# Token-tile order at the joints of a two-block transformer kernel on one Trainium2 core

## The reference

```python
for l in range(DEPTH):          # DEPTH = 2
    h = layer_norm(ALPHA * h + 0.5 * swiglu(h, ffn1_w_gate[l], ffn1_w_up[l], ffn1_w_down[l]), ...)
    h = layer_norm(ALPHA * h + hybrid_mixer(h, ...), ...)       # ends in merged @ w_out
    h = layer_norm(ALPHA * h + 0.5 * swiglu(h, ffn2_...), ...)
```

```python
def modulated_residual(x, c, g, w_mod, b_mod, fn):
    shift, scale, gate = split(silu(c) @ w_mod + b_mod, 3)
    return x + gate * fn(rms_norm_2(x, g) * (1 + scale) + shift)
# swiglu(x) = (silu(x @ w_gate) * (x @ w_up)) @ w_down ; a last rms_norm_2 gives the output
```

## Time and profile before

| | |
|---|---|
| three runs | 3263.46, 3270.26, 3270.85 us; median 3270.26 us |
| profiled execution | 3271.35 us, of which the traced span is 3269.6 us |
| PE busy | 2963.7 us, 91% |
| DVE busy | 1881.6 us, 58% |
| ACT busy | 1355.8 us, 41% |
| mean granted TensorE clock | 0.946 |

### The profile page before, as it was taken

How to read it: one execution, slowest core, us unless ns; L and a number is a source line. 1 busy time by engine, 2 the same in 40 slices (tenths; PEclk the granted TensorE clock), 3 DMA queues, 4 the chain that set the end, 5 groups by cost and what they waited for, 6 DMA issues and landing times.

```text
span 3269.6 us, 41313 instructions
## 1 busy us (share of the span) xinstructions
PE 2963.7 (91%) x15778; PEld 2481.8 (76%) x15778; DVE 1881.6 (58%) x2365; ACT 1355.8 (41%) x1541; POOL 47.6 (1%) x93
## 2 busy tenths in 40 slices
PE   6999898789999989878999799886899999999997
PEld 6987686589899868766987499464777877788776
DVE  6654632176776372325760354142877887778776
ACT  4431211144444122112531154121767666676664
POOL 2000010000000000000000000000000000000000
PEclk9999998889999989989999899977999999999999
DMA  7744321267587332116752365321989988899885
GB/s 255 244 160 148 107 104 54 103 226 247 193 273 245 116 113 103 54 52 222 241 205 103 116 193 165 123 73 48 330 310 334 349 321 314 317 345 341 298 311 213
DMA packets 373331, 659.57 MB, mean 202 GB/s; under 512 B 9034, under 2 KB 195256, under 8 KB 373240
## 3 DMA queue, kind: packets, MB, share of 16 engines
q1 hardware_dynamic: 373240, 658.31, 57.5%
HBM read 657.23 MB, written 1.05 MB: 201 GB/s over the span
## 4 chain that ended last, share of the span: by engine, by line
PE 77%; DVE 9%; issue 5%; DVEq 3%; ACT 2%; PEld 2%; DMA 1%; ACTq 0%; PEldq 0%; SPq 0%
PE banks L649 17%; PE banks L650 17%; PE banks L651 17%; PE banks L1076 9%; PE banks L645 3%; PE banks L1830 3%; DVE ffn_tmp L1557 2%; PE banks L1858 2%; PE banks L1233 2%; PE banks L701 1%; PE banks L773 1%; DVE expert_rest L999 1%; PEld banks L1233 1%; DVEq L1550 1%; PEld banks L1360 1%
## 5 line engine op out<-in xcount | busy, mean ns | idle before, releaser
L649 PE MATMUL banks<-ffn_arena 128*128 128x256 f32 (+1 forms) x3460 | 1169.8, 338 | 69.5 <-DVE expert_rest L999 32.9
L651 PE MATMUL banks<-ffn_arena 128*128 128x256 f32 (+1 forms) x3460 | 1152.7, 333 | 0.0
L649 PEld LDWEIGHTS banks<-ffn_arena 128*128 128x128 f32 x3460 | 664.2, 192 | 142.4 <-issue 45.6
L651 PEld LDWEIGHTS banks<-ffn_arena 128*128 128x128 f32 x3460 | 663.6, 192 | 69.8
L999 DVE TENSOR_TENSOR expert_rest<-expert_raw,ffn_arena 128x2048 fp32r<-128x2048 f32 (+1 forms) x306 | 647.8, 2161 | 118.8 <-ACT ffn_arena L865 113.6
L650 PE MATMUL banks<-ffn_arena 128*128 128x256 f32 (+1 forms) x2200 | 674.0, 306 | 0.0
L865 ACT ACTIVATE ffn_arena<-expert_raw 128x2048 fp32r<-128x2048 f32 (+1 forms) x306 | 538.1, 1809 | 261.2 <-PE banks L651 117.9
L650 PE MATMUL banks<-expert_rest,ffn_arena 128*128 128x512 f32 (+1 forms) x1224 | 468.2, 383 | 0.0
L650 PEld LDWEIGHTS banks<-ffn_arena 128*128 128x128 f32 x2200 | 425.1, 193 | 17.1
L1076 PE MATMUL banks<-HT,panel 128*128 128x256 f32 x1408 | 310.9, 382 | 2.7 <-issue 2.7
L1076 PEld LDWEIGHTS banks<-HT,panel 128*128 128x128 f32 x1408 | 267.8, 192 | 41.8 <-issue 5.9
(11 more groups left out here) (392 smaller groups left out, 2771.4 us busy)
## 6 DMA issues: line engine op xcount, KB each, us to landing
expert_raw<-in_moe_w_gate_dram SPq DMA_DIRECT2D x45, 2048.0 KB, 8.5
expert_raw<-in_moe_w_up_dram SPq DMA_DIRECT2D x45, 2048.0 KB, 7.9
expert_raw<-in_moe_w_down_dram SPq DMA_DIRECT2D x45, 2048.0 KB, 7.9
gate_w<-in_ffn_w_gate_dram SPq DMA_DIRECT2D x55, 1024.0 KB, 5.3
up_w<-in_ffn_w_up_dram SPq DMA_DIRECT2D x55, 1024.0 KB, 5.4
down_w<-in_ffn_w_down_dram SPq DMA_DIRECT2D x55, 1024.0 KB, 5.4
mod_unit<-in_mod_w_dram SPq DMA_DIRECT2D x48, 1024.0 KB, 5.2
panel<-in_w_in_dram SPq DMA_DIRECT2D x24, 2048.0 KB, 8.2
```

Of the source, the lines that this page charges most:

```text
L649: mm(out, w[0], x[0], start=start, stop=False)
L651: return mm(out, w[1], x[0], start=False, stop=stop)
```

## The change

1. `ffn_down_last` takes down panels 9 and 10 together: all of tile 0 for both panels, then all of tile 1. When tile 0's banks are complete it raises a new semaphore, `tile_done`. The output projections have the tile outside the blocks: inside a panel in the mixer and the convolution, outside both panels in attention. The drain after the first of the two panels is gone.
2. `layer_norm`, `residual`, `norm_vec`, `rms_act`, `norm_pe` and the last norm run one tile to its end before the next: tile 0 waits for `tile_done`, tile 1 for `down_done` or `mix_done`. More explicit drains stand between DVE's steps.
3. `mod_pe` writes bank 0 instead of bank 4. Ahead of a mixer it stands between the transposes of the two tiles, after the second FFN behind a wait for tile 0's norm. ACT copies the 24 columns (`mod_act`); the bias is added later, in `norm_start`.
4. `norm_start` (modulation scale and the eight diagonal tiles) moves ahead of the wait for the last products.
5. In an FFN's last step DVE does `panel_low` ahead of `unit_vec`.
6. At the convolution-to-FFN joint ACT copies the gate panel right after `mix_done`, ahead of the squares, and the high part of `HT` is made by halves inside `norm_act`.

```diff
+        def ffn_down_last(pe, n):
+            for t in range(TT):
+                for s, units, weights in ((NS - 2, unit_parts, down_parts), (NS - 1, last_unit_parts, last_down_parts)):
+                    if t == 0:
+                        pe.wait_ge(down_low, n + s + 2)
+                        pe.wait_ge(act_ready, n + s + 1)
+                    for f in range(FB):
+                        last = down_block(units, weights, f, t, False, s == NS - 1 and f == FB - 1)
+                    if t == TT - 1:
+                        last.then_inc(down_done, 1)
+                    elif s == NS - 1:
+                        last.then_inc(tile_done, 1)
...
-        def turn_h(pe, done):
+        def turn_h(pe, done, mod=None):
             for t in range(TT):
+                if t == 1 and mod is not None:
+                    mod_pe(pe, mod)
                 pe.wait_ge(norm_done, done + t + 1)
...
+        def mod_act(act, m):
+            act.wait_ge(mod_col_done, m + 1)
+            act_fn(mod_col[:, bass.ds(m * 24, 24)], banks[:, 0, 0:24], ACT.Copy)
...
         def std_act(act, m, eps):
-            act.wait_ge(var_ready, m)
-            act_fn(spread[:, :, 0], moments[:, :, 1], ACT.Sqrt, bias=eps).then_inc(std_ready, 1)
+            for t in range(TT):
+                act.wait_ge(var_ready, m * TT - TT + t + 1)
+                act_fn(spread[:, t, 0:1], moments[:, t, 1:2], ACT.Sqrt, bias=eps).then_inc(std_ready, 1)
...
-                unit_vec(dve, n, s, FB * SEQ)
                 if final:
                     panel_low(dve, n, s, down_high, down_w, last_down_parts, down_low)
-                else:
+                unit_vec(dve, n, s, FB * SEQ)
...
             for i in range(2):
                 tile = v3(panel_ready(18 + i), 0, 4, D)
-                for k in range(4):
-                    for t in range(TT):
+                for t in range(TT):
+                    for k in range(4):
...
+                    if i == 1 and t == 0:
+                        last.then_inc(tile_done, 1)
             pe.drain().then_inc(mix_done, 1)
+            pe.drain().then_inc(panel_used, 2)
...
                 ffn_pe(pe, n + NS, l * 2 + 1)
+                pe.wait_ge(norm_done, l * 6 + 7)
                 mod_pe(pe, l * 2 + 1)
...
-            def residual(j, src):
+            def residual(j, src, tile=None, whole=None):
                 dve.wait_ge(grow_ready, j + 1)
+                if j + 1 < 4:
+                    norm_start(j + 1)
                 for t in range(TT):
-                    tt(x_norm[:, t, :], src[:, t, :], gate_row[:], ALU.mult)
-                dve.drain()
-                for t in range(TT):
-                    tt(H[:, t, :], H[:, t, :], x_norm[:, t, :], ALU.add)
+                    if t == 0 and tile is not None:
+                        dve.wait_ge(tile_done, tile)
+                    if t == 1 and whole is not None:
+                        dve.wait_ge(*whole)
+                    tt(ffn_tmp[:], src[:, t, :], gate_row[:], ALU.mult)
+                    dve.drain()
+                    tt(H[:, t, :], H[:, t, :], ffn_tmp[:], ALU.add)
+                    dve.drain().then_inc(var_ready, 1)
...
-            norm_act(1)
+            act.wait_ge(mix_done, DEPTH + 1)
             gate_act(act, FFN2, 0)
-            x_high_act(act)
+            norm_act(1, True)
```

More of the change, by code:

```diff
@@ L675, in ffn_down @@
                 for t in range(width // P):
-                    for c in range(2):
-                        last = split_mm(banks[:, 2 * t + c, :], [u[:, f, t * P:(t + 1) * P] for u in units],
-                                        [w[:, f, c * 512:(c + 1) * 512] for w in weights],
-                                        first and f == 0, final and f == FB - 1)
+                    last = down_block(units, weights, f, t, first and f == 0, final and f == FB - 1)
             last.then_inc(down_done, 1)
@@ L689, in ffn_pe @@
             ffn_down(pe, n, 0, first=True)
-            with pe.Fori(2, NS) as s:
+            with pe.Fori(2, NS - 1) as s:
                 ffn_gate(pe, n, s)
@@ L1836, in _ @@
                 tile = v3(panel_ready(6 + i), 0, 4, D)
-                for k in range(4):
-                    for t in range(TT):
+                for t in range(TT):
+                    for k in range(4):
                         for c in range(2):
-                            mm(banks[:, 2 * t + c, :], conv_o[:, 4 * i + k, t * P:(t + 1) * P], tile[:, k, c * 512:(c + 1) * 512],
-                               start=i == 0 and k == 0, stop=i == 1 and k == 3)
-                pe.drain().then_inc(panel_used, 1)
+                            last = mm(banks[:, 2 * t + c, :], conv_o[:, 4 * i + k, t * P:(t + 1) * P], tile[:, k, c * 512:(c + 1) * 512],
+                                      start=i == 0 and k == 0, stop=i == 1 and k == 3)
+                    if i == 1 and t == 0:
+                        last.then_inc(tile_done, 1)
             pe.drain().then_inc(mix_done, 1)
+            pe.drain().then_inc(panel_used, 2)
             norm_pe(1)
@@ L1905, in _ @@
             pe.wait_ge(a_oT_ready, 4)
-            for i in range(2):
-                tile = v3(panel_ready(14 + i), 0, 4, D)
-                for k in range(4):
-                    n = min(P, AW - (4 * i + k) * P)
-                    for t in range(TT):
-                        for c in range(2):
-                            mm(banks[:, 2 * t + c, :], a_oT[0:n, 4 * i + k, t * P:(t + 1) * P], tile[0:n, k, c * 512:(c + 1) * 512],
-                               start=i == 0 and k == 0, stop=i == 1 and k == 3)
-                pe.drain().then_inc(panel_used, 1)
+            tiles = [v3(panel_ready(14 + i), 0, 4, D) for i in range(2)]
+            for t in range(TT):
+                for k in range(KD):
+                    n = min(P, AW - k * P)
+                    for c in range(2):
+                        last = mm(banks[:, 2 * t + c, :], a_oT[0:n, k, t * P:(t + 1) * P], tiles[k // 4][0:n, k % 4, c * 512:(c + 1) * 512],
+                                  start=k == 0, stop=k == KD - 1)
+                if t == 0:
+                    last.then_inc(tile_done, 1)
             pe.drain().then_inc(mix_done, 1)
+            pe.drain().then_inc(panel_used, 2)
             norm_pe(3)
@@ L1961, in _ @@
                 ht_act(act, l * 12 + 4)
+                mod_act(act, l * 2)
                 mixer_act(act, l)
@@ L1984, in norm_act @@
                     last.then_inc(ht_ready, 1)
+                    if high and q % 2:
+                        half = halves(HT)[q // 2]
+                        act.drain()
+                        act_fn(x_parts[0][:, half, :], HT[:, half, :], ACT.Copy).then_inc(x_high, 1)
                 act.wait_ge(grow_done, j + 1)
```

112 lines of the change are left out of this document (56 added, 56 removed).

## The result

| | before | after |
|---|---|---|
| median of the runs | 3268.42 us (3263.46 to 3270.85, 4 runs) | 3229.63 us (3227.9 to 3233.15, 4 runs) |
| profiled execution | 3271.35 us | 3233.15 us, span 3231.3 |
| granted clock, mean | 0.946 | 0.952 |

The ratio is 0.9885, 95% interval 0.9867 to 0.9902: 38.8 us faster. On another chip the same kernel gave 3230.98 us against 3269.72, ratio 0.9883 (0.9868 to 0.9898).

A forecast was written before the change was run, and what follows sets the result against it. TensorE was taken as the bound through most stages (PE 77% of the chain of waits). Joints and tail 40.1, drains +3.4, new wait -0.7, clock -3 gave 39.8 us saved: 3230 us, likeliest case 3216 to 3248, widened to 3213 to 3250.

The forecast's parts named there:

- Part 1: Nine joints and the tail: half of each norm moves under the last products, saving 40.1 us.
- T: At each joint, the moment DVE first reads the finished banks; the prediction counted from it to PE's next-stage first matmul.
- The one term where the edit works against itself: FFN to mixer, twice: modulation columns now stand in the way, so only 1.3 us saved each, 2.6 in all.
- Part 2: Between the two output panels: the drain where PE stood is removed four times, saving 3.4 us.
- Part 3: Last step of five FFNs: PE newly waits for `act_ready`, 0.1 up to 0.4 us each, costing 0.7 us.
- Part 4: Stage starts behind split transposes: some begin at half clock, costing 3 us, of 0 to 8.
- The rival built on the Trainium skill's "VectorE: DVE Perf Modes" (The DRAIN you can't avoid): Joints and tail: added DVE drains at 0.9 us each eat the gain, nothing measurable, 3265 us; chance 0.05.
- B: Inside the FFNs: DVE's modulation work and loads set the pace, losing 17.9 us of savings, 3248 us; chance 0.11.
- D: FFNs' last step: late down-panel loads make PE wait for `act_ready`, eating all 40 us, slower at 3290; chance 0.03.

The follow-up runs named there:

- the extra products: Unread fp32 products of 512 columns filling PE's idle time at mixer to FFN, FFN to FFN and convolution to FFN, against the changed kernel: 3229.26 us.

## Why the prediction was right, and where it was not

**The total** was right (3230 against 3229.63), and its terms deserve a look each, since some errors cancelled.

**Part 1, joints:** 40.1 predicted with the tail, 44.7 measured. The mechanism and the two large blocks held: tile 0's residual 5.4 us early behind an FFN and 6.9 behind mixer and convolution (643.09 to 649.98, 1823.53 to 1830.41), mixer to FFN 10.5 for 11.0, conv to FFN 14.4 for 14.2, FFN to attention 11.4 for 11.0, attention to experts 11.05 for about 11. Part of the sum's error is that T stood 0.17 us behind P at four joints. The norm of a tile was 0.35 us shorter than said, which is most of the 0.5 at mixer to FFN. FFN to mixer came out near at the first site (1.6 for 1.3) by luck: the columns took 8.33 us instead of 7.2, but tile 0's transposes began at P+0.44 and ran at full clock, 1.10 us where I had 1.85. At the second site it was under-sized (3.1 for 1.3), because the columns ran more at full clock (6.83 us). "The one term where the edit works against itself" is confirmed: without the columns these joints are 8.7.

What my account did not show is how much of the gain hangs on the head start. It made three of the four joints with columns look nearly indifferent to the change (1.3 twice and 0.3). Without the columns they would gain 5.1, 5.1, 3.7 and 5.7 us (FFN to mixer twice, FFN to FFN, layer 1 to convolution), and the place given to the columns takes 3.5, 2.0, 2.8 and 1.6 of that back. With the columns in that place and no head start, they are 8 to 10 us longer.

**Part 2, drains:** 3.4 predicted. In the kernel before, the step from one panel to the next costs 0.57 us more than an ordinary step in each mixer, and 0.34 at convolution and attention. In attention nothing of it was saved: the output products take 28.3 us at full clock in the new order too. That makes 1.5 in all. Two readings failed: the ordinary step between two products there is 0.43 us and not 0.24, and two of the four sites cost less than the mixers.

**Part 3, `act_ready`:** 0.7 predicted, 2.5 measured, 0.3 to 0.8 each instead of 0.1. In the first FFN the rest was ready at 209.26, where I had it at 210.1, and PE was at its wait at 209.09, where I had 210.05. The last 48 products had begun at 206.18, and not at 207.3 (207.16 before). So the rest was late by 0.17 us for 0.05, and another 0.15 passes between the rest's end and PE's next product. The swap is worth 0.6 each. Why the wait is 0.8 in layer 1's second FFN is open.

**Part 4, the clock:** 3 predicted. Of the 6.5 us that the stages took back, 2.5 are `act_ready`; with the drains' 1.5 to the good, 5.5 remain. Two parts of it show in products that follow each other without a wait. Attention's output products took 30.27 us for 28.27, 2.0 more by the half clock at their start (last section). The convolution's took 30.15 for 29.59, which with the 0.34 of the drain is 0.9; the granted clock in their first 6 us was 0.59 for 0.74. Neither stands at the start of a stage, where I had placed the loss. There, the traces say this:

| stage | clock in its first 6 us, before and after | length, before and after |
|---|---|---|
| first FFN, layer 0 | 1.00, 0.74 | 191.1, 190.7 |
| mixer, layer 0 | 0.67, 0.59 | 419.1, 419.4 |
| second FFN, layer 0 | 0.54, 0.62 | 191.0, 191.7 |
| first FFN, layer 1 | 0.75, 0.53 | 190.6, 191.7 |
| mixer, layer 1 | 1.00, 0.61 | 419.7, 419.2 |
| second FFN, layer 1 | 0.72, 0.62 | 190.1, 192.0 |
| FFN behind the convolution | 0.55, 0.60 | 189.4, 189.9 |

Behind a mixer and behind the convolution two of the three FFNs began with a higher clock than before, so splitting the transposes cost nothing there. And a lower clock at the start is not always paid: layer 0's first FFN and layer 1's mixer began lower and were not longer. How the remaining 2.6 us divide between clock and waits was not taken apart. That the sum came out right is in part luck: 4.6 us more from the joints stand against 1.9 less from the drains, 1.8 more for the wait and 2.5 more for the rest. Attention's 2.0 us are missing in four profiles of versions with the same attention code, so it is not certain that they belong to the edit.

The Trainium skill, "TensorE: Matmul & The Clock Gate", Part 4 (PE-mode transpose), says that transposes don't engage the full clock. The row of the first joint above (16 transposes in 3.34 us, where 16 at half take 3.67) does not settle it, since they came directly behind other work. The earlier trace rows is the evidence against the rule here: the trace has the clock back at 2072.43, 3.4 us into the transposes and just ahead of the next products (2072.49). The version with the columns first has the same again behind layer 1's first FFN: 16 transposes run from 1059.62 to 1063.27, the granted clock is 0.50 from 1059.6 to 1063.2 and 1.00 from there on, where PE has nothing else. The rival built on the Trainium skill's "VectorE: DVE Perf Modes" (The DRAIN you can't avoid) does not hold for these steps: between the drained steps of the norm stand gaps of 0.07 to 0.2 us, and a tile's four drains fit in the 5.7 us.

**Rivals:** B asked whether the FFNs give the joints' gain back. They gave back a part: the four behind a shortened joint grew by 0.65, 1.1, 1.95 and 0.5 us (table above), 4.3 in sum where the joints ahead of them had saved 19.8, and 2.15 of it are the waits for `act_ready`. Its mechanism, a first step paced by DVE, was there, and took 0.5 us of what the extra products won. D stopped at 2.5 of its 40 us.

## What to carry to other kernels

When a norm is started early on one tile, ask what stands between the two tiles' work on the engine that waits for both: a small product put there can take back most of what the head start brings (here 1.6 to 3.5 of 4 to 6 us). In this kernel the better place was straight behind the last large product, where the clock is still full and nothing is ready yet, in a bank that is free then. Don't count a faster start of a stage before reading the wait and the clock some 20 us into it.

## What the runs showed of the hardware

- One-column fp32 products leave two records a column: 48 took 5.68 us where they were mostly at full clock and 10.24 at half, 0.118 and 0.213 each. They fill PE in the records but did not hold its clock. In the version with the columns first, behind layer 1's first FFN, PE runs nothing else from 1052.9 to 1059.6:

```profile
1052.80:1056.00 3.20, 3.20 (x31) 3.20 (x29) 3.05 (x5) 0.00 (x0) 0.00 (x0) 1.00 0.00 0
1056.00:1059.60 3.60, 3.60 (x20) 3.60 (x20) 2.81 (x5) 0.20 (x1) 0.00 (x0) 0.55 0.00 0
```

- Stages with idle time inside came out some 2 us apart by the same code. Layer 1's mixer took 417.3 and 419.2 us in two profiles of one kernel, and 421.7 in a variant. Attention took 165.3 to 165.6 us in five of the executions profiled and 167.5 to 168.2 in nine, both of the changed kernel among these. The output products took 28.3 us in each of the five and 30.2 to 30.8 in each of the nine. In the changed kernel they start at 2183.4, and the clock shows why:

```profile
2183.00:2185.00 2.00, 1.56 (x2) 0.83 (x3) 0.00 (x0) 0.39 (x2) 0.00 (x0) 0.50 0.00 0
2185.00:2187.00 2.00, 2.00 (x3) 0.66 (x2) 0.00 (x0) 0.00 (x0) 0.00 (x0) 0.50 0.00 0
2187.00:2190.00 3.00, 3.00 (x8) 1.47 (x7) 0.00 (x0) 0.00 (x0) 0.00 (x0) 0.93 0.00 0
```

  So about 2 us of a difference between two versions of this kernel can come from no edit.
- Going round the layer loop took 3.46 us on PE and 3.04 on DVE when the engine had nothing queued. On DVE it counts from the start of the last instruction (3.1 us from 853.25, 3.2 from 858.86), so that a long one hides a part. Behind 48 columns on PE nothing of it showed (852.57 + 7.12 to 859.71). The profile names no releaser for these times; that it is the loop is read from the program, where nothing else lies between.
